# Attention values as the stationary operand, with gate over sum put on the probabilities, in a two-layer decoder trunk

## What is computed

```
s = q @ k_c.T * scale;  p_c = masked_softmax(s, cmp_end <= t);  o_c = p_c @ v_c     # 15 compressed keys
s = q @ k_sel.T * scale; p_s = masked_softmax(s, causal);       o_s = p_s @ v_sel   # br = 0
s = q @ k_win.T * scale; p_w = masked_softmax(s, causal);       o_w = p_w @ v_win   # br = 1
o = gblk[..., 0:1] * o_c + gblk[..., 1:2] * o_s + gblk[..., 2:3] * o_w
...
merged = gate0 * (o_a @ lift_a) + gate1 * (o_b @ lift_b) + gate2 * (o_c @ lift_c)
x = x + merged @ w_out
```

## Time and profile before

| | us |
|---|---|
| median of 3 runs | 2195.62 |
| range of the runs | 2191.7 to 2196.09 |
| the profiled execution | 2195.03 |
| its span, first to last instruction | 2193.2 |

### The profile page before, as it was taken

The page is one execution under the profiler, slowest core; times in us unless marked ns, Lnnn a source line. Parts: engine busy times, 40 slices in busy tenths (PEclk is TensorE's granted clock), DMA queues, the critical chain, the costliest instruction groups (busy, mean ns, idle before and its releaser), DMA issues.

```text
span 2193.2 us, 49711 instructions
## 1 busy us (share of the span) xinstructions
PE 2157.0 (98%) x14494; PEld 1854.9 (85%) x14494; DVE 1250.1 (57%) x2421; ACT 1190.1 (54%) x2283; POOL 1715.0 (78%) x1316
## 2 busy tenths in 40 slices
PE   7999999999999999999999999999999999999999
PEld 6887779999888888888878877899998888888887
DVE  6655447985565655433356555488666665554333
ACT  5455664555555555556554556645555555545565
POOL 6755857888878888888886566778887878888887
PEclk9999999999999999999999999999999999999999
DMA  7433534554444554565563334445554444455555
GB/s 268 148 118 113 173 123 150 183 183 168 163 163 162 166 169 164 172 211 187 190 247 135 124 122 148 144 156 183 178 170 166 162 164 163 165 169 192 191 190 175
DMA packets 100823, 368.20 MB, mean 168 GB/s; under 512 B 11520, under 2 KB 12032, under 8 KB 100480
## 3 DMA queue, kind: packets, MB, share of 16 engines
q1 hardware_dynamic: 97344, 354.46, 48.1%
q10 hardware_dynamic: 3392, 12.66, 1.5%
HBM read 366.03 MB, written 1.05 MB: 167 GB/s over the span
## 4 chain that ended last, share of the span: by engine, by line
PE 94%; issue 2%; DVE 1%; ACT 1%; POOL 1%; POOLq 0%; ACTq 0%; DVEq 0%
PE acc L1101 11%; PE acc L1185 11%; PE acc L1187 11%; PE acc L1186 11%; PE acc L859 6%; PE acc L861 6%; PE acc L860 6%; PE acc L1091 5%; PE acc L1093 5%; PE acc L1092 5%; PE acc L1100 5%; PE aux L1144 4%; PE aux L821 2%; POOL w_lo L464 1%; PE aux L966 1%
## 5 line engine op out<-in xcount | busy, mean ns | idle before, releaser
L464 POOL TENSOR_TENSOR w_lo<-raw,w_hi 128x512 fp32r<-128x512 f32 x1312 | 1714.8, 1318 | 468.6 <-ACT w_hi L495 352.1
L495 ACT ACTIVATE w_hi<-raw 128x512 fp32r<-128x512 f32 x1348 | 844.3, 629 | 704.4 <-PE acc L861 203.0
L1185 PE MATMUL acc<-w_hi,eg 128*128 128x512 f32 x1024 | 406.3, 397 | 0.0
L1187 PE MATMUL acc<-w_hi,eg 128*128 128x512 f32 x1024 | 399.7, 390 | 0.0
L1186 PE MATMUL acc<-w_lo,eg 128*128 128x512 f32 x1024 | 398.8, 390 | 0.0
L1101 PE MATMUL acc<-h_rows,w_hi 128*128 128x512 f32 x1024 | 367.3, 403 | 0.0
L1752 DVE TENSOR_TENSOR eg<-big,eg 128x256 fp32r<-128x256 f32 x256 | 168.8, 659 | 239.6 <-ACT eg L713 233.4
L1091 PE MATMUL acc<-h_rows,w_hi 128*128 128x256 f32 x1024 | 290.9, 284 | 2.1 <-POOL w_lo L464 1.2
L1092 PE MATMUL acc<-h_rows,w_hi 128*128 128x256 f32 x1024 | 289.8, 283 | 0.0
L1093 PE MATMUL acc<-h_rows,w_lo 128*128 128x256 f32 x1024 | 289.8, 283 | 0.0
L1100 PE MATMUL acc<-h_rows,w_lo 128*128 128x256 f32 x896 | 251.9, 281 | 0.0
(11 more groups left out here) (248 smaller groups left out, 2938.1 us busy)
## 6 DMA issues: line engine op xcount, KB each, us to landing
raw<-stream_dram SPq DMA_DIRECT2D x674, 512.0 KB, 3.3
big<-parb_dram ACTq DMA_DIRECT2D x2, 2128.0 KB, 10.3
big<-mem_dram ACTq DMA_DIRECT2D x3, 1024.0 KB, 5.2
big<-pm_dram ACTq DMA_DIRECT2D x2, 768.0 KB, 16.0
big<-parr_dram ACTq DMA_DIRECT2D x2, 640.0 KB, 12.3
X<-x_dram ACTq DMA_DIRECT2D x1, 1024.0 KB, 7.0
out_dram<-X SPq DMA_DIRECT2D x2, 512.0 KB, 3.0
big<-lnrow_dram ACTq DMA_DIRECT2D x2, 256.0 KB, 13.9
```

The source lines that it names most:

```text
L464: nc.gpsimd.tensor_tensor(w_lo[:, k % SLOTS, :], raw[:, k // PER_CHUNK, k % PER_CHUNK, :], w_hi[:, k % SLOTS, :].bitcast(F32), ALU.subtrac ...
L495: nc.scalar.activation(w_hi[:, k % SLOTS, :], raw[:, (k // PER_CHUNK) % RAW, k % PER_CHUNK, :], ACT.Copy).then_inc(hi_ready, 1)
L1185: pe_.matmul(dst, eg[:, q % 2, 0, ts], w_hi[:, slot, :], start=start, stop=False)
L1187: ins = pe_.matmul(dst, eg[:, q % 2, 1, ts], w_hi[:, slot, :], start=False, stop=stop)
```

## The change

The value matmuls swap their operands: 64 columns of values are stationary, the transposed probabilities move, and each head's result (64 x 128, already transposed) goes to one half of the output partitions, so that two heads of a pair stand side by side on the column halves of the array. All of a half's branches (both main ones and the compressed one) are added up in one use of bank 3, `o0` for t = 0 and `o1` for t = 1. For that, gate over sum has to be on the probabilities before their transposes: DVE computes two numbers per unit (`unit_coef`, step `p_coef`), ACT multiplies the two heads of `sring` by them (step `p_scaled`), and PE's transposes wait for `p_scaled` in place of `p_exp`. On ACT the multiplication stands between the two `hi` of the unit. The compressed probabilities get their factor on DVE in unit 0. `combine`, `ot`, the bank uses `oc0`, `oc1`, `br_T0` and `br_T1`, the wait for `o_ready` and the eight transposes of `ot` are gone; ACT's `values_hi(t)` and DVE's `values_lo(t)` read the bank once per half straight into `h_hi` and `h_lo`.

```diff
-                    hi(2, u < len(UNITS) - 1)
+                    if u == PAIRS * 2 + 1:
+                        values_hi(0)
+                    hi(1, u < len(UNITS) - 1)
+                    a.wait("p_coef", u + 1)
+                    for h in range(2):
+                        a.step(nc.scalar.activation(sring[:, u % 2, h, 0:w], sring[:, u % 2, h, 0:w], ACT.Copy,
+                                                    scale=coef[:, 2 * (u % 2) + h:2 * (u % 2) + h + 1]),
+                               "p_scaled" if h == 1 else None)
...
+                    hi(1, u < len(UNITS) - 1)
...
+                def values_hi(t):
+                    a.wait_filled(f"o{t}")
+                    a.step(nc.scalar.activation(h_hi[:, 0:PAIRS, t * P:(t + 1) * P],
+                                                bank(f"o{t}").rearrange("p (j s) -> p j s", j=PAIRS), ACT.Copy, scale=0.5), "o_hi")
...
                 read_gates(5)
-                hi(2)
-                for i in range(2):
-                    hi_T(f"br_T{i}", 2 * i, 2, 0.5)
-                hi(10)
+                values_hi(1)
+                hi(12)
...
-                    e.wait("p_exp", u + 1)
+                    e.wait("p_scaled", u + 1)
...
-                    for h in range(2):
-                        for c in range(t + 1):
-                            at = (2 * j + h) * DK
-                            g = j // 2
-                            ins = pe_.matmul(bank(use)[:, at:at + DK], pT[:, u % 2, h * (t + 1) + c, :],
-                                             zkv[:, c, 3 + 2 * br, g * DK:(g + 1) * DK], start=(c == 0), stop=(c == t))
+                    for c in range(t + 1):
+                        for h in range(2):
+                            ins = pe_.matmul(bank(use)[h * DK:(h + 1) * DK, j * P:(j + 1) * P],
+                                             zkv[:, c, 3 + 2 * br, g * DK:(g + 1) * DK], pT[:, u % 2, h * (t + 1) + c, :],
+                                             start=first and c == 0, stop=(br == 1 and c == t), skip_group_check=True)
...
-                        fill(pe_.matmul(bank(f"oc{u - 2}"), pcT[:, u - 2, :], vblk, start=True, stop=True), f"oc{u - 2}")
-                take(2)
-                e.wait("o_ready")
-                rows_T(["br_T0", "br_T1"], ot)
-                take(10)
+                        for pair in range(PAIRS):
+                            pe_.matmul(bank(use)[:, pair * P:(pair + 1) * P], vblk[:, pair * P:(pair + 1) * P], pcT[:, t, :],
+                                       start=False, stop=False, skip_group_check=True)
+                take(12)
...
+                def unit_coef(u):
+                    t, br, j = UNITS[u]
+                    v = coef[:, 2 * (u % 2):2 * (u % 2) + 2]
+                    d.wait("p_exp", u + 1)
+                    d.step(V.reciprocal(v, sums[:, (t * 2 + br) % 2, 2 * j:2 * j + 2]))
+                    d.step(stt(v, ng[:, t, 6 * j + 1 + br:6 * j + 6:3], 1.0, v, ALU.add, ALU.mult), "p_coef")
+
+                def values_lo(t):
+                    d.wait("o_hi", t + 1)
...
+                    if u == 2 * PAIRS:
+                        values_lo(0)
                     d.wait_filled(use)
                     n = 2 * (t + 1)
                     d.step(V.tensor_copy(pT[:, u % 2, 0:n, :], bank(use)[:, 0:n * P].rearrange("p (n s) -> p n s", n=n)), drains=use)
+                    if u + 1 < len(UNITS):
+                        unit_coef(u + 1)
```

More of the change, by code:

```diff
@@ L89 @@
         USES += [(f"s{_u + 2}", _u % 2)]
-    if _u % PAIRS == 0:
-        USES += [(f"o{_u // PAIRS}", 3)]
-    USES += {1: [("pc_T", 2)], 2: [("oc0", 2)], 3: [("oc1", 2)]}.get(_u, [])
-USES += [("br_T2", 0), ("br_T0", 1), ("br_T1", 2)]
+    if _u % (2 * PAIRS) == 0:
+        USES += [(f"o{_u // (2 * PAIRS)}", 3)]
+    USES += {1: [("pc_T", 2)]}.get(_u, [])
+USES += [("br_T2", 0)]
 USES += [(f"mg_T{i}", (i + 3) % 4) for i in range(4)] + [(f"xa_T{i}", (i + 3) % 4) for i in range(4)]
@@ L195, in trunk @@
         memx, xn, junk = (region(n, T * D, T, D) for n in ("memx", "xn", "junk"))
-        mk, mv, zq, sg, ot, xo, tmp = (region(n, T * 512, T, 512) for n in ("mk", "mv", "zq", "sg", "o", "xo", "tmp"))
+        mk, mv, zq, sg, xo, tmp = (region(n, T * 512, T, 512) for n in ("mk", "mv", "zq", "sg", "xo", "tmp"))
         mkT = region("mkT", XH * MEM, XH, MEM)
@@ L317, in trunk @@
             x_sq=3, x_mean=3, x_sqrt=3, xn_ready=2,
-            hi_T=26, yrows_ready=1,
+            hi_T=24, yrows_ready=1,
             mk_mean=1, mk_sqrt=1, mk_n=1,
@@ L323, in trunk @@
             cs_ready=1, cs_exp=1, pc_ready=1,
-            s_ready=len(UNITS), p_exp=len(UNITS), o_ready=1, merged_ready=2,
+            s_ready=len(UNITS), p_exp=len(UNITS), p_coef=len(UNITS), p_scaled=len(UNITS), o_hi=T, merged_ready=2,
             xq_rows=1, xq_square=T,
@@ L837, in rows_there @@
                             e.wait("yrows_ready")
+                        elif tag == "br" and kt < PAIRS:
+                            e.wait_drained("o1")
                         else:
@@ L991, in _ @@
                     e.wait_drained(f"p_T{u}")
[L992 to L993 removed]
+                    use = f"o{t}"
+                    first, last = (br, j) == (0, 0), (br, j) == (1, PAIRS - 1)
+                    g = j // 2
+                    if first:
                         e.wait_bank_free(use)
[L995 to L1001 removed]
+                    for c in range(t + 1):
[3 more added lines that the diff above has]
+                                             start=first and c == 0, stop=(br == 1 and c == t), skip_group_check=True)
+                    if last:
                         fill(ins, use)
@@ L1481, in _ @@
                 d.step(V.tensor_tensor(scf, scf, cmb, ALU.subtract), "cs_ready")
-                def combine(use, t, k, weights, first, done=None):
-                    d.step(V.reciprocal(coef, weights))
-                    d.step(stt(coef, ng[:, t, k:24:3], 1.0, coef, ALU.add, ALU.mult))
-                    d.wait_filled(use)
-                    dst = (ot if first else tmp)[:, t, :].rearrange("p (h c) -> p h c", h=8)
-                    d.step(V.tensor_tensor(dst, bank(use).rearrange("p (h c) -> p h c", h=8),
-                                           coef.unsqueeze(2).broadcast_to((P, 8, DK)), ALU.mult), drains=use)
-                    if not first:
-                        d.step(V.tensor_tensor(ot[:, t, :], ot[:, t, :], tmp[:, t, :], ALU.add), done)
+                def unit_coef(u):
[6 more added lines that the diff above has]
+                    d.wait("o_hi", t + 1)
+                    ts = slice(t * P, (t + 1) * P)
+                    d.step(stt(h_lo[:, 0:PAIRS, ts], bank(f"o{t}").rearrange("p (j s) -> p j s", j=PAIRS), 0.5,
+                               h_hi[:, 0:PAIRS, ts].bitcast(F32), ALU.mult, ALU.subtract), drains=f"o{t}")
+                d.wait_drained("zg")
+                unit_coef(0)
                 unit_scores(1)
-                d.wait_drained("zg")
                 for u, (t, br, j) in enumerate(UNITS):
                     use = f"p_T{u}"
+                    if u == 2 * PAIRS:
+                        values_lo(0)
                     d.wait_filled(use)
@@ L1506, in _ @@
                         d.step(V.tensor_reduce(cmx, scf, AX.X, ALU.add))
-                        d.step(V.tensor_scalar(cmx, cmx, 1e-30, None, ALU.max), "pc_ready")
+                        d.step(V.tensor_scalar(cmx, cmx, 1e-30, None, ALU.max))
+                        d.step(V.reciprocal(cmx, cmx))
+                        for c in range(T):
+                            d.step(stt(cmx[:, 8 * c:8 * c + 8], ng[:, c, 0:24:3], 1.0, cmx[:, 8 * c:8 * c + 8], ALU.add, ALU.mult))
+                        d.step(V.tensor_tensor(scf, scf, cmb, ALU.mult), "pc_ready")
                     if u == 1:
@@ L1515, in _ @@
                         lo_T("yrows_ready", 6, 2, src=yT)
-                    if j == PAIRS - 1:
-                        combine(f"o{u // PAIRS}", t, 1 + br, sums[:, (t * 2 + br) % 2, :], False,
-                                "o_ready" if u == len(UNITS) - 1 else None)
+                values_lo(1)
                 d.wait_block("z_m4")
@@ L1536, in _ @@
                 gate(1, 0, True)
-                for i in range(2):
-                    lo_T(f"br_T{i}", 2 * i, 2, 0.5)
                 gate(2, 0, False)
```

10 lines of the change are left out of this document (2 added, 8 removed).

## The result

The changed kernel takes 2276.7 us (median of 4 runs, 2275.4 to 2278.6) against 2194.3 for the kernel before: 1.038 times as long, with a 95% interval of 1.037 to 1.039. The forecast was 2254 with a range of 2234 to 2278. The direction was right and the time is 23 us longer than forecast, 1.3 inside the slow end of the range. The profiled execution took 2275.7.

What follows compares the result with a forecast made beforehand. The prediction took PE's own list as the bound (busy 2157.0 of 2193.2 us). Per layer 34.2 us lost less 4.7 gained made 29.5, so 59 for two layers on 2195.0: 2254 us, range 2234 to 2278.

Steps and rivals of the forecast that it cites:

- The main step: Every unit: PE's transposes wait for ACT's rounding, then two multiplications, at least 1 us after the piece in most units.
- the multiplication on the path: Each unit, ahead of the transposes: PE stands still 1.69 us (t = 1) or 1.47 (t = 0), 25.3 us per layer.
- four units with gates: Four units per layer: `read_gates` ahead of the rounding delays it, 1.03 us more stall each, 4.1 us per layer.
- the turn: Unit 8, t = 0 to t = 1: PE's values wait for DVE's copy, behind `values_hi(0)`; 4.1 us lost per layer.
- unit 1: Unit 1: five more small DVE operations for compressed probabilities delay its copy; 0.7 us lost per layer, between 0 and 1.3.
- the wait at the end: Behind the loop: the wait for `ot` and its transposes go, 2.7 us gained per layer.
- value matmuls: Unit loop: two halves partly side by side, eight records in 0.49 us, not 0.81; 2.0 us gained per layer.
- Rival 1: Value matmuls: the array's halves run one after the other, eight records in 1.05 us; 10 us more, 2264; chance 0.11.
- rival 4: Unit loop: the granted clock falls in PE's pauses; 2280 if in a fifth of units, 2380 in all; chance 0.05.
- Rival 2: Unit loop: the multiplications wait only for `p_coef`, not the rounding; stall 1.26 us, not 1.69; 2240; chance 0.06.
- rival 3: Unit loop: roundings and PE drift apart, so multiplications finish in time; 2186 with no stall; chance 0.03.
- Rival 5: Behind the loop: `o1` is read late and PE waits ahead of `lift_a0`; 2 x 1.9 us more, 2258; chance 0.05.

Runs made afterwards that it cites:

- the shift: Changed kernel with one rounding fewer ahead of the unit loop and one more in the last unit: 2210.5 us, ratio 1.008.
- the kernel with shift and turn mended: Changed kernel, one rounding moved from ahead of the loop to the last unit, ACT's copy of first values behind unit 8's multiplications: 2202.1 us, ratio 1.0038.
- the halves apart: Changed kernel with the value matmuls of a unit ordered head by head, not block by block: 2275.9 us.

## Why the prediction was right, and where its sizes were off

The main step held and the size is not luck, but the place inside the range is thin: the slow end had been drawn with a part of the clock's rival in it, and 1.3 us are left. By the prediction's own steps, for both layers together:

| step | forecast | measured |
|---|---|---|
| the multiplication on the path | 50.6 | about 55 |
| four units with gates | 8.2 | 7.7 |
| the turn | 8.2 | 8.7 |
| unit 1 | 1.4 | 1.1 |
| the wait at the end | -5.4 | -5.6, of which 1.7 is lost again |
| value matmuls | -4.0 | about -0.5 |
| transposes to the next piece | 0 | 1.6 |
| the clock | 0 | about 14 |
| elsewhere, -3.8 of it ahead of the loops | 0 | -3.5 |

- **The main step held.** The rounding stands between exponential and multiplication and is released by PE's piece. The pauses are 1.84 and 2.05 where the sum said 1.71 and 1.93. The term was mis-sized by the operation itself: it was priced at 0.32 and 0.43 from a scale by a constant, and took 0.394 and 0.500, as long as the exponential of the same size. Both runs that moved the rounding show the mechanism, the shift above all.
- **Gates, turn, end of the loop** came out as worked out, to within 0.6, but for the 1.7 us that are lost again behind the end: the prediction took the gain there as kept, and PE then waits for POOL's low part of a later piece. Of the units with gates, 4 and 12 pause for 2.80 and 3.00, 0.95 more than the others; 0 and 8 for 2.59 and 3.23. At the turn the values start 4.76 and 4.54 after the last matmul, against 4.4 worked out.
- **The value matmuls** are the term that failed most in proportion. Eight records take 0.59 in place of 0.81, a gain of 0.22 where 0.3 was the best case, and four take 0.37 as before, where 0.15 was hoped for. Ahead of them stand 0.32 us in place of 0.24. That longer step into the column form is not in any row of before; it takes back some 0.09 in each of 32 units, 2.8 of the 3.5 us gained at t = 1. The forecast's doubt went the right way, not far enough. Rival 1 is refuted in its price (1.05 for eight) and not in its cause.
- **The clock** was rival 4, with a chance of 0.05, and the sum had it at nothing. It came in part: at 0.50 for some 20 and 17 us of the two loops, about a sixth of them, worth about 14 us counted step by step against the same steps at 1.00, and 11.9 by the run that fills most of the pauses. It is most of the missing 23. The row on which the forecast relied, a stretch with PE busy for 2.28 of 4.00 us at 1.00, has 1.7 us of idle time in all, and so no pause as long as those here. The falls of the changed kernel came at units with pauses of 2.6 us and more (unit 0, 4, 8, 12) and behind the 4 us at the turn, none in a unit with 1.84 or 2.05 alone. A row of pauses isn't needed: the kernel with shift and turn mended has one pause over 1.4 us per loop, 2.59 at unit 0, and the clock fell behind it in the first layer (the first line) and not in the second:

```profile
136.00:141.00 5.00, 5.00 (x19) 3.27 (x18) 3.99 (x10) 3.51 (x10) 2.57 (x2) 0.66 0.34 105
1224.00:1229.00 5.00, 4.83 (x25) 3.41 (x25) 3.64 (x9) 4.65 (x12) 2.98 (x4) 1.00 0.29 105
```

The Trainium skill ("TensorE: Matmul & The Clock Gate", Why this matters for your kernels) asks for no long idle time between bursts of matmuls. The prediction took the turn as the place for it, and the trace agrees: the clock is 0.57 from 194 to 206. The falls behind the pauses of 2.59 to 3.00 us at units 0, 4 and 12 it did not name.

- **Rival 2** (the rounding isn't waited for) and **rival 3** (faster than before) were wrong, by the rows of unit 6. What the prediction held against rival 3, that PE's pauses can't give ACT a lead, was right for this kernel; one rounding less ahead of the loop gives the lead, and then the pauses are gone. What stays is a kernel 0.3% slower (0.2 to 0.4), so rival 3's 2186 was not reached by any version. **Rival 5** was wrong: no wait of PE stands ahead of `lift_a0`.
- **Not seen at all** was how many waits lie under one another. The forecast sized unit 1 at 0.7, which is right beside long pauses and wrong by 3 without them.

What stays open: how much of the 0.37 and 0.59 is overlap of two halves; why the falls of the clock aren't in the same units in each execution (with the halves apart the first came at unit 4 and not at unit 0); and whether it is the operands or the kind of operation that lets a step of DVE pass beside POOL's.

## What to carry to other kernels

An operation put behind another entry of its queue costs what that entry waits for too, not only its own length: here 0.8 to 1.0 us of multiplication cost 1.6 to 1.8, and moving one rounding across the loop's start returned 66 of 82 us. Before such a change is judged, mend the order of the queues that it stands in and look again, because a pause hides the waits beneath it (here 3.8 us at unit 1). Give the clock a term when pauses enter a loop: here those of 2.6 us and more were followed by 1.2 GHz in part of the cases, which cost 12 to 14 us.

## What the runs showed of the hardware

- A scale taken from a column of SBUF costs ACT 0.085 us more per operation than a constant: 394 against 309 ns on 128 columns, 500 against 416 on 256.
- DVE's SCALAR_TENSOR_TENSOR with two operands from SBUF on 128 x 2 elements takes 0.16 us alone and up to 0.97 beside POOL's split of a piece, and ends with it; a RECIPROCAL in its place takes 0.166 in every unit. A TENSOR_SCALAR with one tensor operand (L1523, 128 x 16) took 1.28 beside a split and ended 0.04 behind it.
- Work that nobody reads can pay: 80 records more on PE in its pauses made the kernel 11.9 us faster, by the clock.
- A matmul behind a change from full width to column halves starts 0.32 us after the last one's start, where it was 0.24 without that change.
